# Two transformer blocks: second experts in 32-row blocks, recurrence's scores once a chunk, attention's products by height

## The reference

```python
def mlstm_chunk(state, xs):                        # once a chunk and direction
    ...
    wts = jnp.exp(d - m_t[..., None]) * jnp.einsum('bhtd,bhsd->bhts', q, k)
    num = jnp.einsum('bhts,bhsv->bhtv', wts, v) + decay[..., None] * jnp.einsum('bhtd,bhdv->bhtv', q, C)
    ...
# mla_attention: 4 heads, query and key of 128 (nope) + 64 (rope) features
    s = jnp.einsum('bhqd,bhkd->bhqk', qb, kh) * scale   # causal, then softmax, then @ v
# hierarchical_moe: top-2 of 8 experts in the best of 4 groups
    hid = jax.nn.silu(xb @ w_gate[e]) * (xb @ w_up[e])
    y = hid @ w_down[e]                                  # times the row's weight, added to its row
```

## Time and profile before

| | us |
|---|---|
| three runs | 4232.98, 4239.25, 4239.27; median 4239.25 |
| the profiled execution, its own time | 4232.68 |
| its span, first to last instruction | 4231.0 |
| busy in the span: PE / DVE / ACT / POOL | 3884.8 (92%) / 1745.0 (41%) / 1457.1 (34%) / 607.2 (14%) |
| mean granted PE clock | 0.956 |
| recurrence, about | 1086 to 1222 |
| latent attention, about | 2862 to 3330 |
| routing and first loads | 3560 to 3628 |
| second experts, up products | 3628 to 4207 |
| after the last up product | 4207 to 4231 |

### The profile page before, as it was taken

How to read it: one execution, slowest core, us unless ns; L and a number is a source line. 1 busy time by engine, 2 the same in 40 slices (tenths; PEclk the granted TensorE clock), 3 DMA queues, 4 the chain that set the end, 5 groups by cost and what they waited for, 6 DMA issues and landing times. The chain is left out here.

```text
span 4231.0 us, 53763 instructions
## 1 busy us (share of the span) xinstructions
PE 3884.8 (92%) x17943; PEld 2433.4 (58%) x17961; DVE 1745.0 (41%) x3722; ACT 1457.1 (34%) x3251; POOL 607.2 (14%) x777
## 2 busy tenths in 40 slices
PE   6999999799879977999999899969999897899998
PEld 4677667455764425777776677745666453333333
DVE  1343344566555560111111488773333445333332
ACT  1122121455444411111111566753333223344443
POOL 0000000100430011111110011110000001333332
PEclk8999999899989968999999899989999998899999
DMA  6221221222534566665654222132231234688863
GB/s 232 79 84 68 94 80 59 78 83 84 160 127 156 181 249 235 199 198 177 214 166 144 69 67 65 56 99 65 60 100 40 98 126 161 213 292 284 284 204 74
DMA packets 228403, 582.04 MB, mean 138 GB/s; under 512 B 28394, under 2 KB 99178, under 8 KB 212382
## 3 DMA queue, kind: packets, MB, share of 16 engines
q1 hardware_dynamic: 176702, 395.92, 27.2%
q0 software_dynamic: 51552, 184.18, 14.5%
HBM read 437.79 MB, written 142.12 MB: 137 GB/s over the span
## 5 line engine op out<-in xcount | busy, mean ns | idle before, releaser
L2145 PE MATMUL out_psO<-out_w,out_mixT 128*128 128x512 f32 x1024 | 452.3, 600 | 3.0 <-ACT out_mixT L2116 1.6
L878 PE MATMUL inp_psU<-inp_w,inp_hT 128*128 128x512 f32 (+3 forms) x1376 | 420.8, 464 | 0.0
L4015 PE MATMUL moe_psU<-moe_wu,moe_xT 128*64 x768 | 344.3, 602 | 6.0 <-issue 5.2
L4017 PE MATMUL moe_psU<-moe_bu,moe_xT 128*64 128x512 f32 x768 | 344.3, 601 | 0.0
L878 PEld LDWEIGHTS inp_psU<-inp_w,inp_hT 128*128 128x128 f32 x1376 | 256.0, 190 | 152.7 <-issue 122.4
L2145 PEld LDWEIGHTS out_psO<-out_w,out_mixT 128*128 128x128 f32 x1024 | 193.9, 192 | 237.3 <-issue 237.1
L874 PE MATMUL inp_psU<-inp_hT,inp_w 128*128 128x256 f32 x1088 | 241.2, 381 | 9.5 <-DVE inp_tm L680 4.5
L2638 PE MATMUL moe_psG<-moe_xT,moe_g_w 128*128 128x256 f32 x1024 | 234.2, 382 | 4.2 <-DMA moe_u_w<-in_w_up 4.2
L3364 PE MATMUL inp_psU<-inp_hT,inp_w 128*128 128x256 f32 x1024 | 231.0, 381 | 2.7 <-DMA inp_wg<-in_lru_wx 2.7
L2638 PE MATMUL moe_psG<-moe_xT,moe_u_w 128*128 128x256 f32 x1024 | 231.5, 379 | 0.0
L874 PEld LDWEIGHTS inp_psU<-inp_hT,inp_w 128*128 128x128 f32 x1088 | 205.9, 191 | 40.6 <-issue 3.9
(11 more groups left out here) (668 smaller groups left out, 6683.9 us busy)
## 6 DMA issues: line engine op xcount, KB each, us to landing
moe_wu<-in_w_up SPq DMA_DIRECT2D x32, 2048.0 KB, 8.4
moe_g_w<-in_w_gate SPq DMA_DIRECT2D x16, 2048.0 KB, 8.6
moe_u_w<-in_w_up SPq DMA_DIRECT2D x16, 2048.0 KB, 13.5
moe_d_w<-in_w_down SPq DMA_DIRECT2D x16, 2048.0 KB, 10.3
moe_wd<-in_w_down SPq DMA_DIRECT2D x32, 1024.0 KB, 12.7
mod_w<-in_w_ada SPq DMA_DIRECT2D x24, 1024.0 KB, 6.9
inp_mod_w<-in_w_mod SPq DMA_DIRECT2D x16, 1024.0 KB, 4.9
xn<-out_xn POOLq DMA_DIRECT2D x32, 512.0 KB, 3.8
```

Source lines behind the costliest of these rows:

```text
L878: mm = pe.matmul(psU[:, u % NB, 0:n], hT[:, par, k, j * P:(j + 1) * P], w[:, k, lo:lo + n], start=(k == 0), stop=(k == KD - 1))
L2145: mm = pe.matmul(psO[:, j, h, :], mixT[:, j, k, :], out_weights.half[k // 4][:, k % 4, h * BANK:(h + 1) * BANK], start=(k == 0), stop=(k = ...
L4015: pe.matmul(psU[0:HALF, p, :], xT[:, p, k, 0:HALF], wu[:, bass.ds(slot, 1), k, :].rearrange("p a n -> p (a n)"), start=(k == 0), stop=(k = ...
L4017: mm = pe.matmul(psU[HALF:P, p, :], xT[:, p, k, HALF:P], bu[:, p, k, :], start=(k == 0), stop=(k == KD - 1), tile_position=(0, HALF))
```

## The change

Three edits, independent of each other.

1. Recurrence: the scores are made in the first 16 visits only, which between them see each chunk once. ACT copies psS into the chunk's place in kT (`keep_scores`), and DVE reads them there, in this visit and in the other direction's.
2. Attention: all 128-row products of a tile come first, then all its 64-row products.
3. Second experts: blocks of 32 rows, a table of 160, so 40 units of four blocks; four lanes of 32 columns; up products 256 wide (gate and up of half the inner width f), the host lays the weights out so. Lanes 1 to 3 read copies, single buffered, in 12 DVE copies of 128x1024 (up), five ACT copies and one DVE copy of 128x1024 (down). One word holds the experts of a unit (`unit_experts`). SP no longer waits for landings; DVE waits for the landing of the unit's last expert (`weights`) and tells ACT. Two buffers for gathered rows instead of four: POOL gathers unit u+2 once the rows of u are transposed, then scatters u-1. The order of PE in a unit: turn(u+1,0), lift(0,0), lift(0,1), lift(1,0), turn_hidden 0, lift(1,1), lower 0, turn_hidden 1, turn(u+1,1), lower 1.

```diff
-BLOCKS2 = 2 * SEQ // HALF + EXPERTS2
-PAIRS2 = BLOCKS2 // 2
+LOT = 32
+LOTS = P // LOT
+BLOCKS2 = 2 * SEQ // LOT + EXPERTS2
+UNITS2 = BLOCKS2 // LOTS
...
+                if i >= NEW:
+                    return
                 pe.wait_ge(q_landed[c], 32)
                 if i:
-                    pe.wait_ge(weighted, i)
+                    pe.wait_ge(scores_kept, i)
...
+            def keep_scores(u):
+                i = u - U0
+                act.wait_ge(scored, i + 1)
+                act.activation(kT[:, chunk(u) - SKIP, :, :], psS[:, :].rearrange("p (h t) -> p h t", h=H), ACT.Copy).then_inc(scores_kept, 1)
...
+                if u < U0 + NEW:
+                    keep_scores(u)
...
-                dve.wait_ge(scored, i + 1)
+                dve.wait_ge(scores_kept, min(i + 1, NEW))
                 if i >= 2:
                     dve.wait_ge(valued, i - 1)
-                dve.tensor_tensor(Wt[:, u % 2, :, :], E[:, u % 2, :, :], psS[:, :].rearrange("p (h t) -> p h t", h=H), ALU.mult
-                                  ).then_inc(weighted, 1)
+                dve.tensor_tensor(Wt[:, u % 2, :, :], E[:, u % 2, :, :], kT[:, chunk(u) - SKIP, :, :], ALU.mult).then_inc(weighted, 1)
...
-                for c0 in range(0, W, 2 * BANK):
-                    parts = [(half, c, min(BANK, W - c)) for half, c in enumerate((c0, c0 + BANK)) if c < W]
-                    for half, c, m in parts:
-                        pe.matmul(flat[:, at + c:at + c + m], qn[j][:, t * P:(t + 1) * P], kn[j][:, c:c + m],
-                                  start=True, stop=False)
-                    for half, c, m in parts:
-                        rows = slice(ROPE * half, ROPE * half + ROPE)
-                        mm = pe.matmul(flat[:, at + c:at + c + m], qr[j][rows, t * P:(t + 1) * P], kr[j][rows, c:c + m],
-                                       start=False, stop=True, tile_position=(ROPE * half, 0))
+                parts = [(c // BANK % 2, c, min(BANK, W - c)) for c in range(0, W, BANK)]
+                for half, c, m in parts:
+                    pe.matmul(flat[:, at + c:at + c + m], qn[j][:, t * P:(t + 1) * P], kn[j][:, c:c + m],
+                              start=True, stop=False)
+                for half, c, m in parts:
+                    rows = slice(ROPE * half, ROPE * half + ROPE)
+                    mm = pe.matmul(flat[:, at + c:at + c + m], qr[j][rows, t * P:(t + 1) * P], kr[j][rows, c:c + m],
+                                   start=False, stop=True, tile_position=(ROPE * half, 0))
...
+            ch.done(dve.tensor_scalar(block_expert[:, :, :].rearrange("p u g -> p (u g)"), psB[:, 0:BLOCKS2], float(E - 1), None, ALU.min))
+            ch.done(dve.tensor_tensor(block_expert[:, :, :], block_expert[:, :, :], place_of[:, :].unsqueeze(1).to_broadcast([P, UNITS2, LOTS]), ALU.mult))
+            ch.done(dve.tensor_reduce(unit_sum[:, :], block_expert[:, :, :], AX, ALU.add))
+            ch.done(dve.tensor_copy(unit_experts[:, :], unit_sum[:, :]))
...
+        bu = s.sb("bu", [P, LOTS - 1, FB, KD, 2 * P])
+        bd = s.sb("bd", [P, LOTS - 1, FB, D])
...
-
-            for e in range(WB):
-                sp.wait_ge(ring.first[e], 32)
-                sp.sem_inc(ready, 1)
             with sp.Fori(1, EXPERTS2 // WB) as i:
                 for j in range(WB):
                     e = i * WB + j
                     free = sp.value_load(done_by[0:1, bass.ds(e - WB, 1)], min_val=1, max_val=NU)
                     sp.wait_ge(lowered, free)
                     sp.sem_inc(passed, 1)
-                    ring.load(sp, e, j, landed[j])
-                    sp.wait_ge(landed[j], i * 32)
-                    sp.sem_inc(ready, 1)
...
-                if late(u, 1) and (not isinstance(u, int) or u + XB - 1 < NU):
-                    gather(u + (XB - 1), (j - 1) % XB)
+                if not isinstance(u, int) or u + XB < NU:
+                    gather(u + XB, j % XB)
...
+            def lift(u, p, slot, f, q):
+                pe.wait_ge(up_copied, u * 4 + (2 * f + q + 1))
+                pe.wait_ge(xT_ready, u * 2 + (q + 1))
+                if q == 0 and late(u, 1):
+                    pe.wait_ge(mixed, u * 2 - 1 + f)
+                for k in range(4 * q, 4 * q + 4):
+                    for g in LANES:
+                        c = slice(g * LOT, (g + 1) * LOT)
+                        w = wu[:, bass.ds(slot, 1), f, k, :].rearrange("p a n -> p (a n)") if g == 0 else bu[:, g - 1, f, k, :]
+                        mm = pe.matmul(psU[c, f, 0:2 * P], xT[:, p, k, c], w, start=(k == 0), stop=(k == KD - 1), tile_position=(0, g * LOT))
+                if q:
+                    mm.then_inc(made, 1)
...
+            def turn_hidden(u, f):
+                pe.wait_ge(mixed, u * 2 + (f + 1))
+                if late(u, 1):
+                    pe.wait_ge(hT_ready, u * 2 - 1 + f)
+                pe.transpose(psH[:, f, 0:P], h[:, f, :], K["ident"][:, :]).then_inc(h_turned, 1)
...
+                slot = slot_of(experts_of(pe, u), 0)
+                if follows(u):
+                    turn(u + 1, 1 - p, 0)
+                lift(u, p, slot, 0, 0)
+                lift(u, p, slot, 0, 1)
+                lift(u, p, slot, 1, 0)
+                turn_hidden(u, 0)
+                lift(u, p, slot, 1, 1)
+                lower(u, slot, 0)
+                turn_hidden(u, 1)
+                if follows(u):
+                    turn(u + 1, 1 - p, 1)
+                lower(u, slot, 1)
...
+                for g in range(1, LOTS):
+                    ins = copy_down(slots[g - 1], 0, g)
+                ins.then_inc(down_copied, 1)
+                copy_down(slots[0], 1, 1)
...
+            def copy_up(slots, f, q):
+                for g in range(1, LOTS):
+                    c = slice(4 * q, 4 * q + 4)
+                    ins = dve.tensor_copy(bu[:, g - 1, f, c, :].rearrange("p k n -> p (k n)").unsqueeze(1),
+                                          wu[:, bass.ds(slots[g - 1], 1), f, c, :].rearrange("p a k n -> p a (k n)"))
+                ins.then_inc(up_copied, 1)
...
+            def copy_last(slot):
+                dve.tensor_copy(bd[:, LOTS - 2, FB - 1, :].unsqueeze(1), wd[:, bass.ds(slot, 1), FB - 1, :]).then_inc(last_copied, 1)
...
+            def weights(experts):
+                last = experts >> (5 * (LOTS - 1))
+                for j in range(WB):
+                    dve.wait_ge(landed[j], ((last + (WB - j)) >> 2) * 32 + 1)
+                dve.sem_inc(unit_ready, 1)
...
+                mix(u, 0)
                 if late(u, 1):
-                    give(u - 1, 1 - p)
-            copy_up(0, 0)
+                    give(u - 1, (j - 1) % 2)
+                copy_last(slot_of(here, LOTS - 1))
+                mix(u, 1)
+                if follows(u):
+                    weights(experts)
+                    copy_all_up(experts)
```

More of the change, by code:

```diff
@@ L3741, in _ @@
             for e in range(SLOTS2):
-                ring.load(sp, e, e, ring.first[e])
+                sp.sem_inc(ring.landed[e], 1)
+                ring.load(sp, e, e)
         @block.gpsimd
@@ L4003, in body @@
+                if f:
+                    mm.then_inc(lowered, 1)
             def body(u, j):
                 p = j % 2
[L4005 to L4011 removed]
@@ new lines, in silu, with keep_hidden @@
+            def silu(u, f):
+                act.wait_ge(made, u * 2 + (f + 1))
+                if late(u, 1):
+                    act.wait_ge(mixed, u * 2 - 1 + f)
+                act.activation(sg[:, f, :], psU[:, f, 0:P], ACT.Silu).then_inc(silued, 1)
+            def keep_hidden(u, f):
+                act.wait_ge(h_turned, u * 2 + (f + 1))
+                if late(u, 1):
+                    act.wait_ge(lowered, u)
+                act.activation(hT[:, f, :], psH[:, f, 0:P], ACT.Copy).then_inc(hT_ready, 1)
@@ L4068, in _ @@
-            copy_down(0, 0)
-            evacuate(0, 0)
+                experts = experts_of(act, u)
+                slots = [slot_of(experts, g) for g in range(1, LOTS)]
+                act.wait_ge(unit_ready, u + 1)
+                if late(u, 1):
+                    act.wait_ge(lowered, u)
+                for g in range(1, LOTS):
+                    ins = copy_down(slots[g - 1], 0, g)
+                ins.then_inc(down_copied, 1)
+                copy_down(slots[0], 1, 1)
+                silu(u, 0)
@@ L4108, in _ @@
+            experts = experts_of(dve, 0)
+            weights(experts)
+            copy_all_up(experts)
             units(dve, body)
-            give(NU - 1, 1)
+            give(NU - 1, (NU - 1) % 2)
 def hybrid_blocks(nc, A, out):
```

263 lines of the change are left out of this document (118 added, 145 removed).

## The result

The changed kernel runs in 4128.3 us (median of 4, 4126.45 to 4130.1) where the kernel before, beside it, ran in 4239.26: the ratio is 0.9735, 95% interval 0.9722 to 0.9748, so 111 us or 2.6% less. The profiled execution has a span of 4124.8 us for 4231.0, 106.2 less; the median of before lay 6.6 us above its profiled execution and that of after 1.9 above its own, which is the rest. The prediction was 4147 in a range of 4120 to 4205.

The account below looks back on a forecast made before the run. PE was taken to bound the recurrence, latent attention and second experts. Gains of 11, 9 and 72 us, together 92, taken from 4239.25 gave 4147 us, range 4120 to 4205.

Parts of the forecast that it names:

- PE alone: Rival, second experts: a unit takes 12.4 us without waits, both small gains come in full; 4127 or 4123 us; chance 0.15.
- Unit on PE: Second experts: products 10.30 us, ten transposes 1.09, six changes of form 0.9; a unit of 12.3 to 12.4 us.
- The unit's waits: Second experts: of 0.48 us waiting a unit, mostly for weights behind SP's serial wait, 0.4 us is kept.
- P = 12.8: Second experts: predicted mean time from one unit to the next, in us, with 0.4 us of waiting included.
- The 4 us given back: Second experts: deducted from a gain of 76 us for a late unit needing three experts and busier DMA engines.
- Tail: After the last up product: 24.0 us less one down group of 3.4, so 20.6 us.
- the 72 of the sum: Second experts' predicted gain in us: end at 4155 for 4231, 76 less the 4 given back.
- Recurrence: Scores dropped from 16 late visits: 0.69 us each after 0.2 lost to uncovered DVE and POOL; 11 us, bounds 6 and 14.
- Attention: Latent attention: 32 alternations of tile height saved at 0.29 us each; 9 us, bounds 5 and 10.
- the 0.09 for the 128-row ones: Latent attention: the 128-row products' share, in us, of an alternation's predicted 0.29 us cost.
- POOL held by the copies: Rival, second experts: POOL's gather waits until DVE's burst of copies ends, P about 14, 4194 us; chance 0.20.
- slower by the scatters, or by PE's instructions: Rival, second experts: scatters waiting on each other, or 45 ns PE instructions, set the pace; 4248 us for scatters; chance 0.10.

Follow-up runs that it names:

- c_experts: The kernel before with the second experts' edit alone: 4147.3 us for 4234.6, ratio 0.9795.
- b_height: The kernel before with the attention's edit alone (loop over pairs of banks taken out of the scores): 4221.9 us for 4234.6, ratio 0.9974.
- one_piece: The changed kernel with a unit's down products behind the next unit's up products and all its transposes in one piece: 4276.7 us for 4234.4, ratio 1.0109.

## Why the prediction was right, and where it was off

**Forecast and size.** Faster, inside the range, by 111 us where 92 was said. The time lies near the rival "PE alone", which gave 4127 and 4123, but not by its mechanism: that rival had no waits left and both small gains in full, and neither was so. The sizes of the two small edits were off in opposite directions (11 said and 7.4 measured, 9 said and 12.7 measured) and cancel by luck; most of the surplus over the forecast is the experts'. 4.8 of the 111 us come with the medians, of which that of before lay 6.6 us over its profiled execution.

**Unit on PE.** 12.3 to 12.4 was said, 12.38 came: four lanes do run at once, and six changes of form cost 0.99 us (12.38 less 10.30 and 1.09) for the 0.9 said. This carried the forecast.

**The unit's waits.** 0.4 us was kept; 12.64 less 12.38 is 0.26 (6 us over the stage against P = 12.8). The reason given, SP's serial wait, isn't borne out: put back into the changed kernel, it cost nothing. The 66.1 us of DVE's wait named SP's queue as the releaser, and I took the queue for the cause. SP passed on a landing, and asks for the next expert 0.9 us behind it; what share of the kernel before's 0.48 us this makes stays open. So the 0.4 was a fair size for a reason that wasn't shown.

**The 4 us given back** for a late unit and busier DMA engines weren't needed as a term of their own: the waits there are in the mean. The DMA share was said to become 0.86 or a little less; it became 0.78.

**Tail.** 20.6 us was said from the end of the last up product, some 17.8 came. The sum took off one down group, 3.4 us; the trace shows another path. POOL scatters the rows of the last unit but one, drains, and scatters the last:

```profile
4106.52 1.57 POOL L3981 DMA_INDIRECT out_rows<-moe_y,moe_at_out  x1 [10.75 <-DVE moe_y L4123]
4116.07 0.18 POOL L3975 COPY moe_at_out<-row_table 128x1 int32<-128x1 int32 x1 [7.98 <-issue]
4117.09 1.57 POOL L3981 DMA_INDIRECT out_rows<-moe_y,moe_at_out  x1 [0.84 <-POOL moe_at_out L3975]
```

From that first scatter to the end it is 18.3 us; in the kernel before 18.2 (4212.83 to 4231.0). The drain between them holds POOL 9.69 us (10.03 before), to 4115.98, though the last outputs are ready at 4113.04. What changed is that the first of these scatters is issued before the end of the last up product and not 5.7 us after it. The drain ends 2.9 us after the outputs are ready, and no run took it out.

Together these make the experts' part 84.5 us in the two profiled executions (603.1 to 518.6), and 87 us in `c_experts`, for the 72 of the sum: 6 from the mean interval, 3 from the tail, and the 4 given back.

**Recurrence.** 11 was said, 7.4 came, between the bounds of 6 and 14. The step that was mis-sized is the 0.2 us a visit that I allowed for what PE had covered; it was 0.38 (3.50 less 3.12). DVE became the bound at 3.50 us a visit, not 3.3, as the text feared of DVE's weighting while POOL works, but mostly at a small instruction (L1813); the weighting itself was held only near the drains (2.06 and 1.28 us for 0.72). These long visits, and the 1.3 us gained in the second visit, the text had not counted.

**Attention.** 9 was said with a bound of 10; the edit alone gave 12.7. The price of an alternation was 0.40 us, not 0.29. The 0.20 for the 64-row products was right. The mis-sized term is the 0.09 for the 128-row ones: it was read from the tile's first group (1.81 us), which follows other full-height products (L3584, 2999.81) and so had no change ahead of it. The second group of the same tile, 3002.90 to 3004.18, has two instructions of 512 columns and two of 128, 1.07 us at 0.429 for 512, and took 1.28: 0.20 over, as `b_height` gave back.

**Rival: POOL held by the copies.** It didn't come: of the 40 gathers 37 took 1.18 to 1.24 us, for 1.00 with no copy beside them, and PE waited 0.6 us for rows. The rule of the Trainium skill (SBUF — State Buffer, the box 'The "DVE blocks DMA" trap (SWDGE)') speaks of descriptors that can't be written during such a copy; the trace here doesn't agree for short copies one behind the other, where 0.22 us is all that a gather lost. In the kernel before the one copy of 2.3 us did hold POOL.

**Rival: slower by the scatters, or by PE's instructions.** Neither: 5 scatters waited for the one before. PE took 27 ns an instruction in the up products without a gap. But POOL's queue could have turned the result, by its order: in `one_piece` the same four lanes lost 148 us.

## What to carry to other kernels

Cost a change of tile form by the same work with one change less, and count how many pieces of full-width work a unit has: here a pair of changes was 0.30 to 0.40 us, and two pieces for three gave 0.37 in a quiet unit. Read such a price from a group that has another form both ahead of it and behind it. On an in-order queue such as POOL's, put what the next unit needs (the gather) ahead of what waits for the last one (the scatter), and check when DVE gives the outputs: one step of that order was 139 us. When an engine is taken off the path, read the small instructions and drains that it had covered, not only the busy sums; and a releaser named in a wait is where the signal came from, which need not be what was late.

## What the runs showed of the hardware that was not expected

- A DVE step on 128x4 elements took 0.78 us for 0.16 while POOL passed over 128x512 in SBUF, and ended with it; a DVE weighting of 128x512 beside two such passes took 2.06 us for 0.72. With POOL's pass moved, POOL itself took 1.48 us for 1.05 beside DVE's 128x512 weighting. Which of the two waits depends on which began first in these rows.
- Twelve DVE copies of 128x1024 in a row (7.48 us) let a gather of POOL through in 1.22 us; one of 128x4096 made a scatter 3.19 us for 1.60.
- Four column lanes took eight instructions (four loads, four products) in 0.215 us, 27 ns each, in the up products of a whole stage (4105.10 to 4105.31, 4105.53, 4105.75), with PE busy 98.8% of the stage.
- An alternation of 128-row and 64-row products cost 0.40 us in each of three widths of tile, half of it in either group.
- A drain of POOL behind a scatter took 9.69 us (10.03 in the kernel before) and, in the changed kernel, ended 2.9 us after the outputs of the next scatter were ready.
- PE's register load of one word took 0.3 us in the kernel before and mostly 1.0 to 1.2 in the changed one (1.09 at 3845.75); why is open.
